# New time tables for the mixer of a streaming encoder step, with its channel layer norm rewritten

## The chip, the core and the metric

The kernel runs on one core of a Trainium2 chip. The metric is the device time of one execution, in microseconds (us). The kernel before took 3596.52 us, the median of three runs (3595.49 to 3606.69). One more execution was recorded by the profiler; the views below are of it.

## The reference, cut to what matters

```python
xn = rmsnorm(x) * norm_mix                     # 1024 prompt rows + 64 sample rows, 1024 wide, float32
u, p, q, gates = split(xn @ w_in)              # 512 | 512 | 512 | 2048
y, h = s5(u)                                   # complex diagonal state space, a scan over time
a = pa * sigmoid(qa),  pa, qa = split(gelu(y) @ w_ssm_glu)
c = depthwise_conv31(p * sigmoid(q)) + conv_b  # causal, 31 taps, 512 channels
b = silu(layernorm(c) * ln_g + ln_b) @ w_conv_out   # the norm runs over the 512 channels
x = x + (sigmoid(gA) * a + sigmoid(gB) * b) @ w_out
# channel mixer, per row of x and head (8): 2 x 128 key scores, top 16 of each, top 16 of their sums,
# softmax weights g_k; then over the 16 chosen experts k of 16384
x = x + sum_k g_k * gelu(u_tab[k] . xn2) * v_tab[k]
out = rmsnorm(x)                               # and the end states of the scan and of the convolution
```

## The kernel before, in words

The rows are taken in four groups (GROUPS): 256 prompt rows and 16 sample rows, so that the mixer works on tiles of 128 channels by 272 columns (time). Each group passes through two jobs.

**The expert job** works on tiles of 128 rows: eight of the prompt and a last one, and for each on pairs of 16-expert lists. Its unit is a turn of four experts, and a turn has two halves of two experts (BATCH = 2). GpSimd (POOL) issues one indirect DMA per expert slot (L1510: 128 rows of 8 KB, that is u_tab and v_tab of the chosen expert, into one of eight slots of rows). VectorE (DVE) forms the dot product (L1383), ScalarE (ACT) takes its gelu, multiplies by the softmax weight and writes a diagonal matrix (L915, L918, L922), and TensorE (PE) adds diag x rows into ps_acc (L765), which frees the slot (semaphore slot_free). DVE also finds the top 16 for the pair to come (choose, L1327 to L1359). A full group is 64 turns, 128 halves.

**The mixer job** makes a group's rows. Weights come as slabs of 512 KB through a ring of four that SP loads; a product (L593) is eight matmuls of 128x272 into one of two banks ps_a, emptied by ACT, or of three banks ps_v, emptied by DVE. Its pieces, in the order of the list PIECES: xn (transposes of the normed rows), u, cq and cp (the convolution's two inputs), s (into the scan), y (out of it, into the single bank ps_y), gate (16 products, ACT's sigmoid), glu, mean and var (the layer norm's two sums by matmul), cout, out, rows, q and score. A table names the half in which PE issues each piece (first dict of a Plan) and the half in which DVE, ACT or POOL take their steps (second dict): turn_in and scan (DVE), turn_back (POOL), gelu (ACT, from ps_y), tap (DVE, one of the 31 taps of the convolution on four channel tiles, L1228), centre, square, eps, root, scale, swish. Before, an emptying by ACT stands in the same half as its product.

The first group's mixer stands alone: the opening, OPEN = 60 halves without expert work (table OPENING). The mixer of each later group is laid beside the expert halves of the group before it (table STEADY; beside() calls mix() in every half). In a half PE issues its mixer piece and then the slots of two experts; ACT does its batch of two experts and then its mixer steps; DVE does its mixer steps and then the dots. Every engine runs its stream in this written order, so a wait of one step holds all that stands behind it.

The layer norm before: PE sums, DVE subtracts the mean (L1275), ACT squares (L866), PE sums again, DVE adds eps (L1279), ACT takes the root (L869), DVE the reciprocal (L1282) and multiplies (L1284); ACT's sigmoid of the scaled and shifted value goes to sq (L873), DVE repeats scale and shift (L1290) and multiplies both into cs (L1293, L1294), which cout reads.

Of the kernel before, what the change touches and what calls it, by code (L numbers as in the profile page):

```python
# [11 lines left out]
P = 128  # L12
# [18 lines left out]
TAPS = 31  # L31
# [51 lines left out]
class Plan:  # L83

    def __init__(self, pe, other, streamed):
        self.pe, self.other = pe, other
# [17 lines left out]
    def due(self, step, h):  # L104
# [6 lines left out]
     "s": [10, 12, 14, 16], "y": [14, 16, 18, 20],  # L111
     "gate": [13 + m for m in range(10)] + [31 + m for m in range(6)], "glu": [23 + j for j in range(DT)],
     "mean": [32], "var": [34], "cout": [38, 39, 40, 41], "out": [43 + j for j in range(DT)],
     "rows": [52, 53, 54], "q": [51 + m for m in range(2 * HEADS)],
     "score": [52 + m for m in range(2 * HEADS)]},
    {"cp": [7, 9, 11, 13], "turn_in": [11, 13, 15, 17], "scan": [11, 13, 15, 17], "turn_back": [11, 13, 15, 17],
     "gelu": [15, 17, 19, 21], "tap": [15 + k // 2 for k in range(TAPS)], "glu": [24 + j for j in range(DT)],
     "centre": [33], "square": [33], "eps": [35], "root": [35], "scale": [36], "swish_in": [36], "swish": [37],
     "cout": [39, 40, 41, 42], "rows": [53, 54, 55], "sq": [55], "ms2": [56], "rs": [57],
     "load_x": [60], "sq_next": [64], "ms_next": [65], "norm_next": [66]}, False)  # L120
STEADY = Plan(
    {"xn": [0], "u": [17, 19, 21, 23], "cq": [1, 5, 9, 13], "cp": [3, 7, 11, 15],
     "s": [20, 22, 24, 26], "y": [26, 28, 30, 32],
     "gate": [25 + 2 * m for m in range(10)] + [44] + [61 + 2 * m for m in range(5)],
     "glu": [45 + 2 * j for j in range(DT)],
     "mean": [52], "var": [58], "cout": [71, 73, 75, 77], "out": [80 + 2 * j for j in range(DT)],
     "rows": [95, 97, 99], "q": [96 + 2 * m for m in range(2 * HEADS)],
     "score": [97 + 2 * m for m in range(2 * HEADS)]},
    {"cp": [5, 9, 13, 17], "turn_in": [22, 24, 26, 28], "scan": [22, 24, 26, 28], "turn_back": [22, 24, 26, 28],
     "gelu": [27, 29, 31, 33], "tap": [18 + k for k in range(TAPS)], "glu": [47 + 2 * j for j in range(DT)],  # L130
     "centre": [54], "square": [55], "eps": [60], "root": [61], "scale": [62], "swish_in": [63], "swish": [65],
     "cout": [73, 75, 77, 79], "rows": [97, 99, 101], "sq": [101], "ms2": [102], "rs": [104],
     "load_x": [106], "sq_next": [117], "ms_next": [119], "norm_next": [121]}, True)
# [6 lines left out]
OPEN = 60  # L140
# [32 lines left out]
def program(nc, x_prompt, x_sample, kept, first, slabs, experts, g_ffn, g_final, x2_d, rs_d, score_d, made_d,  # L173
# [5 lines left out]
    with ExitStack() as ctx:  # L179
# [139 lines left out]
        ln_sig = sem("ln_sig")  # L319
# [85 lines left out]
        def _(sp):  # L405
# [74 lines left out]
            for h in range(OPEN):  # L480
# [316 lines left out]
        def _(act):  # L797
# [198 lines left out]
        def _(dve):  # L996
# [221 lines left out]
            def tap(k):  # L1218

                taps = par("conv_w")  # L1220
                for c in range(CT):
                    src, wk = vbuf[:, c, k:k + NC], taps[:, c * TAPS + k:c * TAPS + k + 1]
                    if k == 0:
                        before[c] = mark(dve.tensor_scalar(acc[:, c, :], src, wk, par("conv_b")[:, c:c + 1],
                                                           ALU.mult, ALU.add))
                    else:
                        after(before[c])
                        last = dve.scalar_tensor_tensor(acc[:, c, :], src, wk, acc[:, c, :], ALU.mult, ALU.add)  # L1228
                        if k < TAPS - 1:
                            before[c] = mark(last)  # L1230
                if k == TAPS - 1:
                    last.then_inc(conv_ready, 1)
# [10 lines left out]
            def mix(h, g):  # L1243
# [23 lines left out]
                for tap_k in due("tap", h):  # L1267
                    tap(tap_k)
# [8 lines left out]
                for _ in due("eps", h):  # L1277
                    src = ready(v_at(g, "var"))
                    dve.tensor_scalar(lnr[0][:, 0:NC], src[:, 0:NC], EPS, None, ALU.add).then_inc(v_done, 1)  # L1279
                for _ in due("scale", h):  # L1280
                    dve.wait_ge(std_ready, g + 1)
                    step(dve.reciprocal(lnr[0][:, 0:NC], lnr[1][:, 0:NC]))  # L1282
                    for c in range(CT):
                        last = dve.tensor_tensor(acc[:, c, :], acc[:, c, :], lnr[0][:, 0:NC], ALU.mult)  # L1284
                    last.then_inc(ln_ready, 1)
                for _ in due("swish", h):
                    dve.wait_ge(ln_ready, g + 1)
                    for c in range(CT):
# [160 lines left out]
        def _(pool):  # L1449
# [172 lines left out]
```

## Time and profile before

| | |
|---|---|
| median of three runs | 3596.52 us |
| the profiled execution's own time | 3593.31 us |
| its span | 3591.5 us |
| mean granted TensorE clock | 0.97 of full speed |
| busy: PE, DVE, ACT, POOL | 3193.5, 2417.2, 1431.2, 1381.5 us |
| opening, up to the first expert gather | about 329 us |

A page of the profile gives busy times of the engines, the share of the 16 DMA engines in 40 slices, the groups of instructions that cost most, and who waited for whom. The windows view gives the same for chosen stretches; the timeline lists instructions in order, with the idle time in front of each and what ended it in brackets.

### The profile page before, as it was taken

To read this page: it belongs to the slowest core of one execution; us is meant where nothing else is said; L and a number is where in the kernel's file an instruction comes from. 1 tells how busy PE (TensorE), PEld (TensorE's weight loads), DVE (VectorE), ACT (ScalarE), POOL (GpSimd) and SP (SyncE) were. 2 spreads that over 40 slices of the span, in tenths; PEclk is the share of its full clock that TensorE was granted. 3 is DMA by queue.
4 is the path that set the end of the run, shared out by engine and by line. 5 is a ranking of instruction groups with operands and counts; after the bars stand their busy time and mean duration, and the time that the engine had idled before them with its cause. 6 is when DMAs were issued, how large, how long until landed. Compare 5 with 4: busy or idle time off the path is not lost.

```text
span 3591.5 us, 33867 instructions
## 1 busy us (share of the span) xinstructions
PE 3193.5 (89%) x10052; PEld 1819.9 (51%) x10052; DVE 2417.2 (67%) x5507; ACT 1431.2 (40%) x4220; POOL 1381.5 (38%) x1231
## 2 busy tenths in 40 slices
PE   7889998999999998999999998989999877777776
PEld 6676555555555555555655555555555322222232
DVE  6633579767656678867656588867656666666664
ACT  4312444554334345554334345553333333333332
POOL 2101345333333445434333345434343444444443
PEclk9899999999999999999999999999999999999999
DMA  4256999999999999999999998999999999999998
GB/s 135 71 170 230 382 418 343 381 415 369 418 411 408 399 411 345 392 392 392 419 405 398 401 407 336 401 386 400 418 411 400 416 419 420 396 420 401 419 381 347
DMA packets 232072, 1336.42 MB, mean 372 GB/s; under 512 B 27664, under 2 KB 49296, under 8 KB 92624
## 3 DMA queue, kind: packets, MB, share of 16 engines
q0 software_dynamic: 156672, 1140.92, 78.1%
q1 hardware_dynamic: 62992, 179.96, 13.5%
q10 hardware_dynamic: 12224, 13.38, 1.0%
q8 instruction: 80, 1.31, 0.1%
q14 instruction: 104, 0.85, 0.1%
HBM read 1310.93 MB, written 23.23 MB: 371 GB/s over the span
## 4 chain that ended last, share of the span: by engine, by line
PE 58%; DMA 21%; DVE 8%; ACT 8%; issue 4%; POOL 1%; POOLq 0%; SPq 0%; ACTq 0%; DVEq 0%
PE ps_acc L765 32%; DMA rows<-in_experts,idx 20%; PE ps_a L593 14%; PE ps_v L593 4%; PE ps_a L668 3%; DVE rows L1383 3%; ACT uy L824 2%; POOL rows L1510 1%; DVE va L1228 1%; ACT coef L918 1%; ACT diag L922 1%; PE ps_a L695 1%; PE ps_y L635 1%; ACT L915 1%; PE ps_a L672 1%
## 5 line engine op out<-in xcount | busy, mean ns | idle before, releaser
L765 PE MATMUL ps_acc<-rows,diag 128*128 128x512 f32 x4352 | 2030.9, 614 | 292.0 <-ACT diag L922 289.3
L1510 POOL DMA_INDIRECT rows<-in_experts,idx x1088 | 1257.3, 1156 | 1894.5 <-PE ps_acc L765 1529.2
L1383 DVE CUSTOM_DVE_ANT_0 rows<-rows,xn 128x1024 f32<-128x1024 f32 x1088 | 1330.1, 1232 | 827.4 <-DMA rows<-in_experts,idx 812.7
L765 PEld LDWEIGHTS ps_acc<-rows,diag 128*128 128x128 f32 x4352 | 831.2, 196 | 1335.8 <-issue 848.0
L915 ACT ACTIVATE act_v<-dots 128x2 f32<-128x2 f32 x544 | 109.6, 201 | 1161.2 <-DVE dots L1383 1150.0
L922 ACT ACTIVATE diag<-pk,coef 128x128 f32<-128x128 f32 x1088 | 377.2, 394 | 17.7
L593 PE MATMUL ps_a<-xnT,ring 128*128 128x272 f32 x1536 | 375.8, 400 | 0.9 <-ACT xnT L812 0.7
L593 PEld LDWEIGHTS ps_a<-xnT,ring 128*128 128x128 f32 x1536 | 297.4, 194 | 93.3 <-issue 34.4
L918 ACT ACTIVATE coef<-act_v,soft 128x1 f32<-128x1 f32 x1088 | 261.4, 287 | 17.8
L593 PE MATMUL ps_a<-gates,ring 128*128 128x272 f32 x1024 | 247.7, 395 | 4.4 <-issue 3.5
L1228 DVE SCALAR_TENSOR_TENSOR va<-va,pk 128x302 f32<-128x302 f32 x480 | 240.2, 564 | 1.9
L593 PEld LDWEIGHTS ps_a<-gates,ring 128*128 128x128 f32 x1024 | 194.7, 191 | 67.4 <-issue 29.1
L855 ACT ACTIVATE gates<-ps_a,pk 128x272 f32<-128x272 f32 x64 | 31.2, 488 | 281.0 <-PE ps_a L593 280.8
L593 PE MATMUL ps_v<-uy,ring 128*128 128x272 f32 x512 | 126.9, 398 | 7.6 <-DVE uy L1294 7.6
L668 PE MATMUL ps_a<-xnT,ring 128*128 128x272 f32 x512 | 130.3, 399 | 2.2 <-DVE xnT L1304 1.2
L915 ACT ACT_TABLE_LOAD x99 | 127.0, 1283 | 6.8 <-DVE dots L1383 5.1
L593 PEld LDWEIGHTS ps_v<-uy,ring 128*128 128x128 f32 x512 | 98.7, 193 | 33.5 <-DVE uy L1294 8.1
L668 PEld LDWEIGHTS ps_a<-xnT,ring 128*128 128x128 f32 x512 | 94.5, 190 | 30.9 <-issue 11.5
L1383 DVE DVE_READ_ACCUMULATOR2_ANT dots<- 128x1 f32 x1088 | 88.9, 82 | 0.0
L892 ACT ACTIVATE sig<-ps_a 128x272 f32<-128x272 f32 x64 | 25.3, 395 | 159.3 <-PE ps_a L593 159.1
L824 ACT ACTIVATE uy<-ps_a 32x68 f32<-32x68 f32 x256 | 56.0, 219 | 81.7 <-PE ps_a L593 78.9
L1487 POOL TENSOR_TENSOR rs<-rs,half 128x3 f32<-128x3 f32 x4 | 3.6, 889 | 196.7 <-DVE rs L1178 196.6
(227 smaller groups left out, 2258.9 us busy)
## 6 DMA issues: line engine op xcount, KB each, us to landing
ring<-in_slabs SPq DMA_DIRECT2D x256, 512.0 KB
rows<-in_experts,idx POOLq DMA_INDIRECT x1088
ring<-made_slabs SPq DMA_DIRECT2D x24, 512.0 KB
sc<-score_rows SPq DMA_DIRECT2D x68, 128.0 KB
score_rows<-gp ACTq DMA_DIRECT2D x32, 256.0 KB
xt<-in_x_prompt SPq DMA_DIRECT2D x4, 1024.0 KB, 14.4
x_rows<-xt ACTq DMA_DIRECT2D x4, 1024.0 KB, 10.8
x2t<-x_rows SPq DMA_DIRECT2D x8, 512.0 KB
```

Source lines behind the costliest of these rows:

```text
L593: last = pe.matmul(out[:, 0:N], w, rhs[:, k, :], start=(k == 0), stop=(k == kt - 1))
L635: last = pe.matmul(out, w, hst[:, t % 2, c, i, 0:NK], start=False, stop=(c == 1))
L668: last = pe.matmul(out[:, 0:N], ring[:, slot, k * P:(k + 1) * P], merged[:, k, :], start=(k == 0), stop=(k == DT - 1))
L672: pe.matmul(out[:, n:n + width], xt[0:width, t, j * P:(j + 1) * P], eye[0:width, 0:width], start=False, stop=False, skip_group_check=True)
L765: ins = pe.matmul(ps_acc[:, h, :], diag[:, slot, :], rows[:, slot, D + h * 512:D + (h + 1) * 512], start=False, stop=False, skip_group_che ...
L824: last = act.activation(o, x, func)
L915: act.activation(act_v[:, cols], dots[:, cols], ACT.Gelu).then_inc(gelu_done, 1)
L918: act.activation(coef[:, s:s + 1], act_v[:, s:s + 1], ACT.Copy, scale=soft[:, n % 2, s:s + 1]).then_inc(coef_done, 1)
L922: act.activation(diag[:, s % RING, :], shape, ACT.Copy, scale=coef[:, s:s + 1]).then_inc(diag_done, 1)
L1228: last = dve.scalar_tensor_tensor(acc[:, c, :], src, wk, acc[:, c, :], ALU.mult, ALU.add)
L1383: ins = dve.tensor_tensor_reduce(rows[:, slot, 0:D], rows[:, slot, 0:D], xn[:, :], 1.0, 0.0, ALU.mult, ALU.add, dots[:, s:s + 1])
L1510: pool.indirect_dma_start(out=rows[:, slot, :], out_offset=None, in_=experts, in_offset=bass.IndirectOffsetOnAxis(ap=idx[:, a, k:k + 1], a ...
```

## The change

Both tables are written anew, and four pieces of code change with them.

- **lag**: with lag = 1 (STEADY) ACT's emptyings of ps_a stand one half after their product; the opening keeps 0. xn is left as it was.
- **tap** works in 32 units: a unit is two taps on two of the four channel tiles, the first 16 units on tiles 0 and 1, the rest on tiles 2 and 3. The count of instructions stays at 124 for a group.
- **layer norm**: POOL raises var + eps to the power -0.5 (one TENSOR_TENSOR on 128x302, with half, which holds -0.5); ACT's root and DVE's reciprocal go. ACT's Silu writes cs directly, in eight instructions (four tiles, prompt and sample columns apart); ACT's four sigmoids and DVE's twelve instructions go.
- **tables**: opening: y three halves apart (was two), 13 gates ahead of glu and 3 behind (was 10 and 6), mean and var between the glu products, OPEN = 59, all from out on one half earlier. Groups: u, s and y spread over halves 9 to 36 (was 17 to 32), taps over halves 11 to 46 without the four halves of turn_in (was 18 to 48 without a gap), mean at 48 (was 52), cout at 68 (was 71), q at 93 (was 96).
- SP loads the scores of the first two lists two and four halves behind their last score piece, one list at a time (was both at the sixth q piece), and the first x2 rows at the ninth q piece (was the eighth).

```diff
-     "s": [10, 12, 14, 16], "y": [14, 16, 18, 20],
+     "s": [10, 12, 14, 16], "y": [15, 18, 21, 24],
...
-                if h == OPENING.pe["q"][5]:
-                    for b in range(2):
+                for b in range(2):
+                    if h == OPENING.pe["score"][2 * b + 1] + 2:
                         sp.wait_ge(score_out[b], 32)
                         load_scores(0, b)
-                if h == OPENING.pe["q"][7]:
+                if h == OPENING.pe["q"][8]:
...
             def mix(h, g):
-                at, due = plan(g).at, plan(g).due
-                for _ in at("xn", h):
+                due = plan(g).due
+
+                def at(piece, h):
+                    return plan(g).at(piece, h - plan(g).lag)
+
+                for _ in plan(g).at("xn", h):
...
-                for _ in due("root", h):
-                    v_emptied(v_at(g, "var"))
-                    act.activation(lnr[1][:, 0:NC], lnr[0][:, 0:NC], ACT.Sqrt).then_inc(std_ready, 1)
-                for _ in due("swish_in", h):
+                for _ in due("swish", h):
+                    act.wait_ge(y_done, CT * (g + 1) + 2)
                     act.wait_ge(ln_ready, g + 1)
                     for c in range(CT):
-                        act.activation(sq[:, c, :], acc[:, c, :], ACT.Sigmoid, bias=par("ln_b")[:, c:c + 1],
-                                       scale=par("ln_g")[:, c:c + 1]).then_inc(ln_sig, 1)
+                        out, shape = by_step(cs[:, c, :]), (par("ln_b")[:, c:c + 1], par("ln_g")[:, c:c + 1])
+                        act.activation(out[:, :, 0:KP], in_time(acc[:, c, 0:NP]), ACT.Silu, bias=shape[0], scale=shape[1])
+                        act.activation(out[:, :, KP:NK], in_time(acc[:, c, SOFF:NC]), ACT.Silu, bias=shape[0],
+                                       scale=shape[1]).then_inc(cs_ready, 1)
...
+            def tap(unit, g):
+                taps, (two, first) = par("conv_w"), divmod(unit, 16)
+                if first == 0:
+                    emptied(v_at(g, "cp", 2 * two + 1))
+                for k in range(2 * first, min(2 * first + 2, TAPS)):
+                    for c in (2 * two, 2 * two + 1):
...
+                for _ in plan(g).due("root", h):
+                    pool.wait_ge(var_ready, g + 1)
+                    pool.tensor_tensor(lnr[1][:, 0:NC], lnr[0][:, 0:NC], half[:, 0:1].to_broadcast([P, NC]),
+                                       ALU.pow).then_inc(std_ready, 1)
```

On PE in the opening, from one y piece (L632, L635) to the next, before: the last instructions of a y, two gate products, the next y, which waits for the gelu of the one ahead (y_gelu).

```order
L635 MATMUL ps_y<-hst,rows 128x68 x2
L593 MATMUL ps_a<-xnT,ring 128x272 [waits slab_in3,a_done]
L593 MATMUL ps_a<-xnT,ring 128x272 x7
L593 MATMUL ps_a<-xnT,ring 128x272 [waits slab_in0,a_done]
L593 MATMUL ps_a<-xnT,ring 128x272 x7
L632 MATMUL ps_y<-uy,rows 128x68 [waits wt_done,unrotated,y_gelu]
L635 MATMUL ps_y<-hst,rows 128x68 x2
```

The same place after, where the lines are L635, L638 and L596:

```order
L638 MATMUL ps_y<-hst,rows 128x68 x2
L596 MATMUL ps_a<-xnT,ring 128x272 [waits slab_in1,a_done]
L596 MATMUL ps_a<-xnT,ring 128x272 x7
L596 MATMUL ps_a<-xnT,ring 128x272 [waits slab_in2,a_done]
L596 MATMUL ps_a<-xnT,ring 128x272 x7
L596 MATMUL ps_a<-xnT,ring 128x272 [waits slab_in3,a_done]
L596 MATMUL ps_a<-xnT,ring 128x272 x7
L635 MATMUL ps_y<-uy,rows 128x68 [waits wt_done,unrotated,y_gelu]
L638 MATMUL ps_y<-hst,rows 128x68 x2
```

Between two y pieces there are now three gate products, and no longer two.

On ACT in the opening, from the last two gates ahead of the layer norm's root to the first out piece (L877), before:

```order
L855 ACTIVATE gates<-ps_a,pk 128x272 [waits a_ready] x2
L869 ACT_TABLE_LOAD
L869 ACTIVATE hst<-hst 128x302 [waits v_done]
L855 ACT_TABLE_LOAD
L855 ACTIVATE gates<-ps_a,pk 128x272 [waits a_ready]
L873 ACTIVATE gp<-va,pk 128x302 [waits ln_ready]
L873 ACTIVATE gp<-va,pk 128x302 x3
L877 ACTIVATE gates<-ps_a 128x272 [waits a_ready]
```

And after, from the gates that stand ahead of Silu (L879, L880):

```order
L862 ACTIVATE gates<-ps_a,pk 128x272 [waits a_ready] x2
L879 ACT_TABLE_LOAD [waits ln_ready]
L879 ACTIVATE uy<-va,pk 128x4x64 [waits y_done]
L880 ACTIVATE uy<-va,pk 128x4x4
L879 ACTIVATE uy<-va,pk 128x4x64
L880 ACTIVATE uy<-va,pk 128x4x4
L879 ACTIVATE uy<-va,pk 128x4x64
L880 ACTIVATE uy<-va,pk 128x4x4
L879 ACTIVATE uy<-va,pk 128x4x64
L880 ACTIVATE uy<-va,pk 128x4x4
L862 ACT_TABLE_LOAD
L862 ACTIVATE gates<-ps_a,pk 128x272 [waits a_ready]
```

The root and its table load are gone; eight Silu instructions with a table of their own write uy (cs), and one gate follows them.

On DVE in a later group, a turn_in and scan (rot, rin, into, gp) and what follows, before:

```order
L1197 TENSOR_TENSOR rin<-rot 128x272 [waits v_done]
L1199 TENSOR_TENSOR into<-carry,decay 128x16 [waits unrotated]
L1203 TENSOR_TENSOR rin<-rin,into 128x8x2 [waits v_chain]
L1212 SCALAR_TENSOR_TENSOR gp<-decay,none,rin 128x272 [waits unrotated,v_chain]
L1212 SCALAR_TENSOR_TENSOR gp<-decay,none,rin 128x272
L1228 SCALAR_TENSOR_TENSOR va<-va,pk 128x302 [waits v_chain] x4
L1375 RECIPROCAL inv<-den 128x2 [waits exp_done]
L1376 TENSOR_TENSOR soft<-ex,inv 128x32 [waits v_chain]
L1383 ISA rows,dots<-rows,xn 128x1024 [waits landed0]
```

And after, the same steps of a later group:

```order
L1204 TENSOR_TENSOR rin<-rot 128x272 [waits v_done]
L1206 TENSOR_TENSOR into<-carry,decay 128x16 [waits unrotated]
L1210 TENSOR_TENSOR rin<-rin,into 128x8x2 [waits v_chain]
L1219 SCALAR_TENSOR_TENSOR gp<-decay,none,rin 128x272 [waits score_out1,unrotated,score_out0,v_chain]
L1219 SCALAR_TENSOR_TENSOR gp<-decay,none,rin 128x272
L1386 ISA rows,dots<-rows,xn 128x1024 [waits landed4]
L1386 ISA dots 128x1
L1386 ISA rows,dots<-rows,xn 128x1024 [waits landed5]
L1386 ISA dots 128x1
L1238 SCALAR_TENSOR_TENSOR va<-va,pk 128x302 [waits v_chain] x4
```

Before, a tap (L1228) stood in the same half as each turn_in; now the half goes on with what the expert job has there, and the next unit of taps comes a half later.

## Rows read from the trace of the kernel before

**Rows 1.** The page, part 1: busy us (share of the span) x instructions.

```profile
PE 3193.5 (89%) x10052; PEld 1819.9 (51%) x10052; DVE 2417.2 (67%) x5507; ACT 1431.2 (40%) x4220; POOL 1381.5 (38%) x1231
```

**Rows 2.** Windows: stretch, length, busy of each engine, PE clock, DMA share, GB/s.

```profile
103.00:165.00 62.00, 48.83 (x184) 41.12 (x184) 35.59 (x75) 21.25 (x62) 6.12 (x8) 0.75 0.17 54
...
430.00:530.00 100.00, 95.04 (x297) 54.52 (x296) 73.51 (x175) 40.88 (x132) 41.12 (x36) 1.00 1.01 419
530.00:670.00 140.00, 123.03 (x438) 76.60 (x438) 121.78 (x259) 73.62 (x221) 68.76 (x68) 0.93 0.91 346
...
790.00:850.00 60.00, 52.09 (x151) 29.09 (x150) 41.17 (x95) 29.83 (x66) 21.05 (x20) 0.94 0.92 360
...
2750.00:3570.00 820.00, 617.01 (x1341) 248.96 (x1340) 540.65 (x1215) 264.04 (x877) 375.13 (x312) 0.97 1.00 408
```

**Rows 3.** Timeline of the opening, PE: start, length, instruction [idle before, ended by].

```profile
90.08 7.55 PE L593 MATMUL ps_a<-xnT,ring 128*128 128x272 f32 x32
...
103.19 0.69 PE L632 MATMUL ps_y<-uy,rows 128*128 128x68 f32 x2 [3.83 <-ACT uy L824]
...
108.37 9.97 PE L593 MATMUL ps_a<-xnT,ring 128*128 128x272 f32 x32
123.89 0.69 PE L632 MATMUL ps_y<-uy,rows 128*128 128x68 f32 x2 [5.56 <-ACT uy L824]
...
165.03 2.10 PE L593 MATMUL ps_a<-uy,ring 128*128 128x272 f32 x8 [1.89 <-ACT uy L824]
...
228.34 17.08 PE L593 MATMUL ps_v<-uy,ring 128*128 128x272 f32 x64 [7.63 <-DVE uy L1294]
...
314.43 0.93 PE L695 MATMUL ps_a<-pk,sig 128*128 128x128 f32 x6
...
319.06 0.93 PE L695 MATMUL ps_a<-pk,sig 128*128 128x128 f32 x6
```

**Rows 4.** Timeline of the opening, ACT.

```profile
118.37 0.49 ACT L855 ACTIVATE gates<-ps_a,pk 128x272 f32<-128x272 f32 x1 [3.18 <-PE ps_a L593]
118.88 1.28 ACT L824 ACT_TABLE_LOAD   x1
120.17 3.67 ACT L824 ACTIVATE uy<-ps_y 32x68 f32<-32x68 f32 x16
```

**Rows 5.** Timeline of the opening, DVE.

```profile
73.10 0.44 DVE L1191 TENSOR_TENSOR rot<-ps_v,trig 128x272 f32<-128x272 f32 x1 [1.09 <-PE ps_v L617]
...
76.01 1.46 DVE L1212 TENSOR_TENSOR_SCAN gp<-decay,none,rin 128x272 f32<-128x272 f32 x2
...
221.44 1.62 DVE L1284 TENSOR_TENSOR va<-va,hst 128x302 f32<-128x302 f32 x4
...
318.82 0.30 DVE L1327 MAX8 topv<-sc 128x8 f32<-128x128 f32 x1 [8.31 <-DMA sc<-score_rows]
```

**Rows 6.** Lines of POOL, by form: count | busy us, mean ns | idle before.

```profile
L1467 POOL TENSOR_TENSOR gp<-gp,trig 128x272 f32<-128x272 f32 x16 | 16.8, 1049 | 0.0
...
L1487 POOL TENSOR_TENSOR rs<-rs,half 128x3 f32<-128x3 f32 x4 | 3.6, 889 | 196.7 <-DVE rs L1178 196.6
```

**Rows 7.** Timeline of POOL: the first gather.

```profile
329.28 1.19 POOL L1510 DMA_INDIRECT rows<-in_experts,idx  x1 [17.82 <-DVE idx L1359]
```

**Rows 8.** Waits from 530 to 670 us: total us, times, longest.

```profile
ACT gates L855 <- PE ps_a L593: 31.1, 6, 9.3
...
PE ps_y L632 <- ACT uy L824: 6.8, 3, 2.5
```

**Rows 9.** Waits from 790 to 850 us.

```profile
DVE hst L1282 <- ACT hst L869: 6.7, 1, 6.7
...
DVE va L1290 <- ACT gp L873: 5.2, 1, 5.2
```

**Rows 10.** Lines of DVE: the taps.

```profile
L1228 DVE SCALAR_TENSOR_TENSOR va<-va,pk 128x302 f32<-128x302 f32 x480 | 240.2, 564 | 1.9
```

**Rows 11.** Source view of L1279, eps, in the mixers of groups three and four.

```profile
L1279 DVE TENSOR_SCALAR hst<-ps_v x2: 473/473/473, 1579.6 to 2382.4; 128x302 f32<-128x302 f32 x2
```

More of the change, by code:

```diff
@@ L83, with __init__ @@
 class Plan:
-    def __init__(self, pe, other, streamed):
-        self.pe, self.other = pe, other
+    def __init__(self, pe, other, streamed, lag):
+        self.pe, self.other, self.lag = pe, other, lag
         self.a, self.v, self.slab, self.slabs = {}, {}, {}, []
@@ L110 @@
     {"xn": [0], "u": [1, 2, 3, 4], "cq": [5, 7, 9, 11], "cp": [6, 8, 10, 12],
-     "s": [10, 12, 14, 16], "y": [14, 16, 18, 20],
[L112 to L115, printed above, removed]
-    {"cp": [7, 9, 11, 13], "turn_in": [11, 13, 15, 17], "scan": [11, 13, 15, 17], "turn_back": [11, 13, 15, 17],
[L117 to L120, printed above, removed]
+     "s": [10, 12, 14, 16], "y": [15, 18, 21, 24],
@@ new lines @@
+     "gate": [13 + m for m in range(13)] + [34 + m for m in range(3)], "glu": [26 + j for j in range(DT)],
+     "mean": [29], "var": [32], "cout": [37, 38, 39, 40], "out": [42 + j for j in range(DT)],
+     "rows": [51, 52, 53], "q": [50 + m for m in range(2 * HEADS)],
+     "score": [51 + m for m in range(2 * HEADS)]},
+    {"cp": [7, 9, 11, 13], "turn_in": [11, 13, 15, 17], "scan": [11, 13, 15, 17], "turn_back": [11, 13, 15, 17],
+     "gelu": [16, 19, 22, 25], "tap": [10, 10, 12, 12, 14, 14, 16, 16] + [18 + u // 2 for u in range(24)],
+     "glu": [27 + j for j in range(DT)],
+     "centre": [30], "square": [30], "eps": [33], "root": [33], "scale": [34], "swish": [35],
+     "cout": [38, 39, 40, 41], "rows": [52, 53, 54], "sq": [54], "ms2": [55], "rs": [56],
+     "load_x": [59], "sq_next": [63], "ms_next": [64], "norm_next": [65]}, False, 0)
@@ L121 @@
 STEADY = Plan(
-    {"xn": [0], "u": [17, 19, 21, 23], "cq": [1, 5, 9, 13], "cp": [3, 7, 11, 15],
-     "s": [20, 22, 24, 26], "y": [26, 28, 30, 32],
-     "gate": [25 + 2 * m for m in range(10)] + [44] + [61 + 2 * m for m in range(5)],
+    {"xn": [0], "u": [9, 11, 21, 23], "cq": [1, 5, 13, 17], "cp": [3, 7, 15, 19],
+     "s": [12, 16, 24, 28], "y": [20, 24, 32, 36],
+     "gate": [25 + 2 * m for m in range(10)] + [44, 54] + [61 + 2 * m for m in range(4)],
      "glu": [45 + 2 * j for j in range(DT)],
-     "mean": [52], "var": [58], "cout": [71, 73, 75, 77], "out": [80 + 2 * j for j in range(DT)],
-     "rows": [95, 97, 99], "q": [96 + 2 * m for m in range(2 * HEADS)],
-     "score": [97 + 2 * m for m in range(2 * HEADS)]},
@@ L129 @@
[L129 to L133, printed above, removed]
+     "mean": [48], "var": [54], "cout": [68, 70, 72, 74], "out": [77 + 2 * j for j in range(DT)],
@@ new lines @@
+     "rows": [94, 96, 98], "q": [93 + 2 * m for m in range(2 * HEADS)],
+     "score": [95 + 2 * m for m in range(2 * HEADS)]},
+    {"cp": [6, 10, 18, 22], "turn_in": [14, 18, 26, 30], "scan": [14, 18, 26, 30], "turn_back": [14, 18, 26, 30],
+     "gelu": [21, 25, 33, 37],
+     "tap": [11, 12, 13, 15, 16, 17, 19, 20, 21, 22, 23, 24, 25, 27, 28, 29] + [31 + u for u in range(16)],
+     "glu": [48 + 2 * j for j in range(DT)],
+     "centre": [51], "square": [52], "eps": [57], "root": [57], "scale": [60], "swish": [61],
+     "cout": [70, 72, 74, 76], "rows": [96, 98, 100], "sq": [101], "ms2": [102], "rs": [104],
+     "load_x": [106], "sq_next": [117], "ms_next": [119], "norm_next": [121]}, True, 1)
@@ L139 @@
 SKEW = 4
-OPEN = 60
+OPEN = 59
 ALL_TURNS = TILES * TPAIRS * PTURNS + SPAIRS * PTURNS
@@ L318, in program @@
         neg_rs = sem("neg_rs")
-        ln_sig = sem("ln_sig")
+        var_ready = sem("var_ready")
         cs_ready = sem("cs_ready")
@@ L1216, in _ @@
             before = [0] * CT
[L1218 to L1231, printed above, removed]
+            def tap(unit, g):
[4 more added lines that the diff above has]
+                    for c in (2 * two, 2 * two + 1):
+                        src, wk = vbuf[:, c, k:k + NC], taps[:, c * TAPS + k:c * TAPS + k + 1]
+                        if k == 0:
+                            before[c] = mark(dve.tensor_scalar(acc[:, c, :], src, wk, par("conv_b")[:, c:c + 1],
+                                                               ALU.mult, ALU.add))
+                        else:
+                            after(before[c])
+                            last = dve.scalar_tensor_tensor(acc[:, c, :], src, wk, acc[:, c, :], ALU.mult, ALU.add)
+                            if unit < 31 or k < TAPS - 1:
+                                before[c] = mark(last)
+                if unit == 31:
                     last.then_inc(conv_ready, 1)
@@ L1266, in mix @@
                     scan(t, g)
-                for tap_k in due("tap", h):
-                    tap(tap_k)
+                for unit in due("tap", h):
+                    tap(unit, g)
                 for j in due("glu", h):
```

19 lines of the change are left out of this document (6 added, 13 removed).

## Prediction

> **What bounds the kernel now.** I read the page first [rows 1]: PE is busy for 89% of the span, DVE for 67%. That names no bound, since the stages differ. The windows do [rows 2]. From 430 to 530 us the DMA engines stand at a share of 1.01 with 419 GB/s: the expert gathers and the slabs fill them, and no engine's work counts there. From 2750 us on, where only experts are left, it is the same (1.00): 312 gathers in 820 us are 2.63 us each. So time can be won only where the DMA engines are not full. There are two such places. The first is the opening, up to the first gather at 329.28 us [rows 7]. The second recurs in each of three groups: 530 to 670 us at a share of 0.91, and 790 to 850 us at 0.92. Against 1.01 these lose 140 x 0.10 = 14.0 us and 60 x 0.09 = 5.4 us, 19.4 us a group.
>
> The timelines of the opening say what it waits for: PE, and PE for ACT. In front of a y piece PE stands 3.83 or 5.56 us [rows 3], because ACT first empties the gate ahead (0.49), loads a table (1.28) and does the gelu (3.67) [rows 4]: 0.49 + 1.28 + 3.67 and the hand-overs make 5.56. After it PE is slow: from 103 to 165 us the granted clock is 0.75 in the mean [rows 2], some of it at the lower of the two levels (1.2 and 2.4 GHz). Two gate products took 9.97 us after a 3.83 us idle and 7.55 us before it [rows 3], 2.4 us more, and the y between (103.19 to 108.37, 5.18 us) about double, 2.6 us more. So an idle of that size costs itself and 5.0 us. The idle of 1.89 us at 165.03 cost nothing more: eight instructions took 2.10 us, as fast as any.
>
> **The opening, part by part.** A y now comes every three halves with three gate products between. The gelu starts behind the second, and the third (7.55 / 2, about 3.7 us) covers it but for 5.56 - 3.7, about 1.9 us. The y pieces start behind three gelus, so three idles of 1.9 us; the fourth gelu stands behind the last gate and glu waits the full 5.56 us. Idle before: y 3.83, 5.56, 5.56 (one row stands for two) and glu 1.89, 16.8 us; after 3 x 1.9 + 5.56 = 11.3. The slow spells behind the three long idles go (15.0), one comes behind the glu idle (5.0). Three gates move from behind glu to ahead (11.1).
> First glu: 165.03 - 16.8 + 11.3 - 15.0 + 11.1 = 155.6 us.
> From there to cout 63.3 us before (228.34 - 165.03). Three gates fewer: -11.1. Slow spell: +5.0. The idle ahead of cout, 7.63 us, becomes what the new layer norm leaves open. Behind var PE has one glu and three gates, 4 x 3.7 = 14.8 us. Beside them runs eps (0.47), the power P, four multiplies (1.62) [rows 5], a table load (1.28), which waits for the multiplies, and eight Silus, which I put at 3 us from the gate row of 0.49 for 272 columns, plus 0.4 for hand-overs: P + 6.8. ACT's own way (second last gate emptied, table, Silu) is 3.7 + 7.4 + 0.5 + 1.3 + 3.0 = 15.9. So the idle is 1.1 us up to P = 9 and P - 8 beyond.
> P is the unknown. No row shows a power over 302 columns. The near rows are 0.889 us for a power over 3 columns and 1.049 us for a product over 272 [rows 6]. If all but the product's rate per column is fixed cost, P = 0.9 + 302 x 1.049 / 272 = 2.1 us. If the 3 columns carry the whole, P = 302 x 0.889 / 3 = 89 us. The two rows stand equally near, so I take a value between, 10 us, and keep both ends. Idle 2.1 us, so -5.5.
> First cout: 155.6 + 63.3 - 11.1 + 5.0 - 5.5 = 207.3 us, 21.0 earlier. The couts took 17.08 us for 64 instructions behind the 7.63 us idle, against 7.55 / 32 x 64 = 15.1 [rows 3]; that 2.0 comes back too. From out on nothing changes but SP: the first list's scores are fetched behind the fifth q piece, not the sixth, and a q piece with its score takes 319.06 - 314.43 = 4.6 us. DVE waited for that fetch 8.31 us to 318.82 [rows 5], and the first gather hangs on it [rows 7]. So 4.6 more. The second list's fetch is 9.2 us behind the first, and DVE needs 10.5 us for the first list (318.82 to 329.28), so it is not late. x2's fetch goes later by one q piece and now runs beside gathers; the first landed rows, up to 8 x 2.63 us of them, cover it.
> Opening: 21.0 + 2.0 + 4.6 = 27.6 us. What hides the taps: 32 of 124 stand ahead of the last scan, which can't start before the last s piece ends (99.4, where the 3.83 us idle begins) and takes 4.4 (73.10 to 76.01 + 1.46 [rows 5]). The other 92 at 0.564 us [rows 10] take 52 us, to 156; mean comes behind four glus, near 175.
>
> By the Trainium skill (ScalarE: Activation LUTs, What ACT_TABLE_LOAD costs) a switch of tables costs a drain of 1.38 us behind the load's 1.28. Here the gelu starts 1.29 us behind its load's start [rows 4], so no drain shows. By the page Silu's switch would end 1.4 us later, and the forecast would be 1.4 us more.
>
> **The groups.** From 530 to 670 us ACT waited 31.1 us for gate products of its own half, up to 9.3 at once, and PE 6.8 us for gelus [rows 8]: y, gelu and y two halves apart held each other. With lag 1 a product stands a whole half ahead of its emptying, and y four halves apart, so both waits go. DVE is late next, being 121.78 us busy of 140 [rows 2]. Its expert work is 540.65 / 156 = 3.47 us a half (312 gathers are 156 halves); a tap step adds 4 x 0.564 = 2.26, turn_in with scan 4.4. Halves 18 to 33 before: 16 x (3.47 + 2.26) + 4 x 4.4 = 109.3 us, 6.83 a half. Halves 14 to 30 after, 13 of 17 with a tap unit: 59.0 + 29.4 + 17.6 = 106.0, 6.23 a half. A half lasts (2382.4 - 1579.6) / 128 = 6.27 us [rows 11]. The excess was 16 x 0.56 = 9.0 us and goes to nothing: 9.0 of the 14.0 come back. The rest stays with DVE, which is still nearly full.
> From 790 to 850 us DVE stood 6.7 us for ACT's root and 5.2 for its sigmoids [rows 9], both held behind a gate that PE had still to make. Root and reciprocal go, eps to scale has three halves (18.8 us), Silu needs no DVE. The power holds POOL for P; the gathers behind it wait, but eight slots in flight last 8 x 2.63 = 21 us. I take 3.2 of the 5.4 back. DVE's new wait for the last gate ahead of cout has two halves of slack; behind it stand the dots. 12.2 us a group, 36.6 for three; between 0 and all 19.4.
>
> **Sum.** 3593.3 - 27.6 - 36.6 = 3529.1 against the profiled execution. The median of the runs shown is 3.2 us above it, so 3532 us.
>
> **Rivals.**
> A, only the opening gains. For it: DVE is as full as before, and PE was 123.03 us busy of 140 at a clock of 0.93; a window's loss may be PE's and stay. Against: the waits in rows 8 and 9 are queue waits. 3532 + 36.6 = 3569 us.
> B, slower: the power costs by the column. Place: POOL, in the opening and in front of the gathers in each group. With 89 us, the opening's idle is 81 instead of 2.1 (+79), and each group loses 89 - 21 = 68 us beyond what the slots cover (+204): 3815 us. It decides from P where (P - 10) + 3 x (P - 21) eats the 64 us: P = 34 us, 0.11 us a column. For it: 0.889 us is long for 3 columns. Against: such a time over so few columns looks like fixed cost. The Trainium skill (GPSIMD Engine Reference, 3.1 Elementwise) says to leave elementwise work to VectorE, with 2.6 cycles a column for two inputs; it has no price for a power. Its direction is B's, and the product row, 1.049 us, is all this trace has on it.
> C, three idles of 1.9 us lower the clock as those of 3.83 did: 15 us of the opening's gain stay away, 3547 us. Against it stands the one 1.89 us idle.
> D, the groups get all 19.4 us: 3532 - 21.6 = 3510 us. The wait for PE and for DVE would both have to vanish.
>
> **How the numbers follow.** Forecast 0.54, A 0.17, B 0.11, C 0.10, D 0.08. A measurement can tell 0.3%, 10.8 us, from no change, so below 3585.7 is faster. Forecast, C and D are; of A, 0.01 is lost to a power of 20 to 30 us in it; that and the near side of B give 0.04 for the same, and 0.11 for slower: faster 0.85. The likeliest's own range, with a P of 2 to 20 us and groups of 7 to 17 us each, is 3510 to 3556. The range 3500 to 3585 takes in A, C and D and leaves out B.
>
> **What would show it.** Right: the first gather near 301 us; PE's idles ahead of y near 1.9 us with the gates between at full clock; glu near 156 and cout near 207 us; POOL's power near 10 us; the two stretches at a DMA share of 0.97 or more, and eps steps some 790 us apart instead of 803. Wrong: a power above 34 us; ACT still waiting for ps_a in the groups; a share that stays at 0.91 with DVE full; an idle ahead of cout above 5 us.

## The result: slower, and the profile after

The changed kernel takes 3684.1 us (median of 4 runs, 3679.6 to 3689.0) against 3596.0 (3591.3 to 3606.7): a ratio of 1.024, interval 1.022 to 1.026. The forecast was 3532 us. The profiled execution took 3688.98 us, its span 3687.2.

The page of the changed kernel, parts 1 and 5, with columns as in [rows 1, 10]:

```profile
PE 3178.9 (86%) x10052; PEld 1806.4 (49%) x10052; DVE 2403.1 (65%) x5455; ACT 1447.7 (39%) x4241; POOL 1599.7 (43%) x1235
...
L1238 DVE SCALAR_TENSOR_TENSOR va<-va,pk 128x302 f32<-128x302 f32 x480 | 256.3, 598 | 2.7
L1497 POOL TENSOR_TENSOR hst<-hst,half 128x302 f32<-128x302 f32 x4 | 196.2, 49046 | 78.2 <-DVE hst L1289 78.2
```

Only POOL has much more to do than in [rows 1], 218 us more, and four powers of 49.05 us each are 196 of them. The waits of DVE (total us, times, longest) say who paid:

```profile
DVE rows L1386 <- DMA rows<-in_experts,idx: 824.8, 609, 4.4
DVE va L1295 <- POOL hst L1497: 182.1, 4, 46.5
```

This is how it looks in a group, first on POOL, then on DVE (timelines around 790 us; L1517 is the gather, L1497 the power, L1289 eps, L1295 the scale):

```profile
793.44 0.93 POOL L1517 DMA_INDIRECT rows<-in_experts,idx  x1 [0.31 <-issue]
794.38 49.57 POOL L1497 TENSOR_TENSOR hst<-hst,half 128x302 f32<-128x302 f32 x1
844.15 1.19 POOL L1517 DMA_INDIRECT rows<-in_experts,idx  x1 [0.20 <-issue]
```

```profile
788.43 0.47 DVE L1289 TENSOR_SCALAR hst<-ps_v 128x302 f32<-128x302 f32 x1
...
843.99 1.62 DVE L1295 TENSOR_TENSOR va<-va,hst 128x302 f32<-128x302 f32 x4 [45.56 <-POOL hst L1497]
```

The power begins 5.95 us after eps does. DVE is at the scale at 843.99 - 45.56 = 798.43 us, 4.05 us later: that is all of the power that DVE doesn't wait for there. The stages, as in [rows 2]:

```profile
350.00:370.00 20.00, 8.38 (x41) 6.50 (x40) 9.85 (x32) 2.14 (x5) 7.75 (x8) 0.84 1.01 401
...
390.00:410.00 20.00, 20.00 (x77) 12.80 (x76) 1.36 (x4) 6.48 (x22) 3.75 (x4) 1.00 1.00 401
410.00:430.00 20.00, 20.00 (x74) 12.35 (x73) 16.46 (x35) 8.36 (x27) 13.05 (x7) 1.00 0.80 275
430.00:530.00 100.00, 94.08 (x296) 53.96 (x295) 69.88 (x159) 46.24 (x144) 43.58 (x40) 0.97 0.99 397
530.00:670.00 140.00, 135.51 (x499) 83.76 (x498) 131.54 (x290) 76.51 (x236) 73.29 (x68) 0.99 0.97 395
...
790.00:850.00 60.00, 17.04 (x47) 8.76 (x46) 11.52 (x28) 7.70 (x19) 57.27 (x7) 0.67 0.24 87
```

The crowded stretch of 530 to 670 us has risen from a DMA share of 0.91 to 0.97, as forecast. That of 790 to 850 us has fallen from 0.92 to 0.24: while POOL raises to the power, no gather is issued and every other engine runs dry. Eps steps of the groups stand (2436.8 - 788.4) / 2 = 824.2 us apart, not 790.

The opening on PE, the steps of [rows 3]; below it the first gather on POOL, for [rows 7]:

```profile
100.34 7.55 PE L596 MATMUL ps_a<-xnT,ring 128*128 128x272 f32 x32
109.78 0.44 PE L635 MATMUL ps_y<-uy,rows 128*128 128x68 f32 x2 [1.89 <-ACT uy L827]
...
114.04 13.00 PE L596 MATMUL ps_a<-xnT,ring 128*128 128x272 f32 x48
...
163.95 4.00 PE L596 MATMUL ps_a<-uy,ring 128*128 128x272 f32 x8 [5.56 <-ACT uy L827]
...
199.87 11.16 PE L596 MATMUL ps_a<-xnT,ring 128*128 128x272 f32 x48
252.79 17.29 PE L596 MATMUL ps_v<-uy,ring 128*128 128x272 f32 x64 [41.76 <-ACT uy L880]
```

```profile
350.87 1.19 POOL L1517 DMA_INDIRECT rows<-in_experts,idx  x1 [14.93 <-DVE idx L1362]
```

The idles are the forecast ones, 1.89 and 5.56 us. But the three gate products behind the first idle take 13.00 us, where the same number of instructions, 48, takes 11.16 at 199.87: they ran partly at the lower clock. And cout waits 41.76 us for the layer norm instead of 2.1.

### The profile page after: what moved, and what is told of

Same layout as the page of the kernel before. It is cut to its first block, busy times and chain, and to the rows that moved or that the text cites. A ratio compares the mean times of both kernels' runs of the same rounds, so it can differ in the third digit from the quotient of the medians.

```text
span 3687.2 us, 33829 instructions
## 1 busy us (share of the span) xinstructions
PE 3178.9 (86%) x10052; PEld 1806.4 (49%) x10052; DVE 2403.1 (65%) x5455; ACT 1447.7 (39%) x4241; POOL 1599.7 (43%) x1235
## 4 chain that ended last, share of the span: by engine, by line
PE 50%; DMA 24%; DVE 9%; POOL 7%; ACT 6%; issue 4%; POOLq 0%; SPq 0%; ACTq 0%; DVEq 0%
PE ps_acc L768 27%; DMA rows<-in_experts,idx 23%; PE ps_a L596 12%; POOL hst L1497 5%; DVE rows L1386 4%; PE ps_a L671 3%; PE ps_v L596 3%; POOL rows L1517 2%; DVE va L1238 2%; ACT uy L827 1%; ACT coef L925 1%; PE ps_a L698 1%; ACT diag L929 1%; PE ps_a L675 1%; PE ps_acc L759 1%
## 5 line engine op out<-in xcount | busy, mean ns | idle before, releaser
L1517 POOL DMA_INDIRECT rows<-in_experts,idx x1088 | 1275.7, 1172 | 1805.0 <-PE ps_acc L768 1476.3
L596 PE MATMUL ps_a<-xnT,ring 128*128 128x272 f32 x1536 | 373.6, 398 | 0.9 <-ACT xnT L815 0.7
L596 PEld LDWEIGHTS ps_a<-xnT,ring 128*128 128x128 f32 x1536 | 295.7, 193 | 92.7 <-issue 34.4
L596 PE MATMUL ps_a<-gates,ring 128*128 128x272 f32 x1024 | 248.9, 397 | 18.7 <-ACT sig L899 17.9
L1238 DVE SCALAR_TENSOR_TENSOR va<-va,pk 128x302 f32<-128x302 f32 x480 | 256.3, 598 | 2.7
L596 PEld LDWEIGHTS ps_a<-gates,ring 128*128 128x128 f32 x1024 | 195.3, 192 | 83.6 <-issue 24.7
L1497 POOL TENSOR_TENSOR hst<-hst,half 128x302 f32<-128x302 f32 x4 | 196.2, 49046 | 78.2 <-DVE hst L1289 78.2
L596 PE MATMUL ps_v<-uy,ring 128*128 128x272 f32 x512 | 127.7, 399 | 41.8 <-ACT uy L880 41.8
L596 PEld LDWEIGHTS ps_v<-uy,ring 128*128 128x128 f32 x512 | 99.3, 194 | 68.0 <-ACT uy L880 42.2
L1295 DVE TENSOR_TENSOR va<-va,hst 128x302 f32<-128x302 f32 x16 | 6.5, 469 | 182.1 <-POOL hst L1497 182.1
L596 PE MATMUL ps_a<-uy,ring 128*128 128x272 f32 x256 | 65.9, 401 | 5.6 <-ACT uy L827 5.6
```

The source lines that it names most:

```text
L596: last = pe.matmul(out[:, 0:N], w, rhs[:, k, :], start=(k == 0), stop=(k == kt - 1))
L1497: pool.tensor_tensor(lnr[1][:, 0:NC], lnr[0][:, 0:NC], half[:, 0:1].to_broadcast([P, NC]), ALU.pow).then_inc(std_ready, 1)
L1517: pool.indirect_dma_start(out=rows[:, slot, :], out_offset=None, in_=experts, in_offset=bass.IndirectOffsetOnAxis(ap=idx[:, a, k:k + 1], a ...
```

## Experiments

"Root back" below means one edit on the changed kernel: ACT's Sqrt (it waits for eps) and DVE's reciprocal in place of POOL's power. The edits are shown cut to the lines that matter. The kernel before was measured again beside each set of experiments, so its median moves a little, between 3592.9 and 3596.7 us; ratios are against the one beside it.

**1. Root back.**

```diff
-                    pool.tensor_tensor(lnr[1][:, 0:NC], lnr[0][:, 0:NC], half..., ALU.pow)
+                    act.activation(lnr[1][:, 0:NC], lnr[0][:, 0:NC], ACT.Sqrt)
+                    step(dve.reciprocal(lnr[0][:, 0:NC], lnr[1][:, 0:NC]))
```

> The changed kernel with one thing undone: GpSimd's power over 302 columns goes, ACT takes the square root (waiting for eps) and VectorE the reciprocal; all of the new tables and ACT's silu stay. T1 (the power's price by column, 4 x 49.06 us, of which VectorE waits 182.1 us, is the whole loss): about 3684 - 182 + 4 x 2 (root, table load, reciprocal) = 3500 to 3520 us; both stretches without a hole; VectorE's wait ahead of scale under 5 us. R1 (the new tables themselves cost, the power only fills slack): it stays above 3596 us. R2 (clock falls behind the 1.89 us idles and x2's later fetch cost most of what the opening gains): 3530 to 3560 us, with the first gather near 310 us.

Measured 3507.3 us, 0.977 of the kernel before (0.975 to 0.979). Against 3684.1 the power costs 176.9 us, 44.2 in the mean of four places. The two traces say how it is spread: the first gather comes at 350.87 us with the power and at 310.27 without, 40.6 us, and eps steps of the groups stand 824.2 us apart with it and 776.3 without, 47.9 us a group. (That adds up to 184 us, which is what the two profiled executions are apart; the medians are 177 apart.) R1 of the expectation falls: tables, lag, taps and silu together are good for 85.6 us (3592.9 us for the kernel before).

**2. Root back, x2's rows behind the eighth q piece as before.**

```diff
-                if h == OPENING.pe["q"][8]:
+                if h == OPENING.pe["q"][7]:
```

> As the run before it (root and reciprocal back in place of the power), and x2's rows of the first group fetched behind the eighth q piece, as in the kernel before, not behind the ninth. If the late fetch is what holds ACT 14.5 us and empties VectorE from 390 to 410 us in the changed kernel: 5 to 15 us faster than the run before it, and the wait of ACT for that fetch goes to a few us. If the prediction's view holds (the fetch is covered by landed rows): the same within 3 us.

Measured 3495.6 us (3493.5 to 3498.6) against 3504.9 to 3509.4: 11.6 us for one half's difference, and the prediction's cover is refuted. With the late fetch ACT waited once for it, 14.5 us in the changed kernel (the line below) and 15.2 us in experiment 1:

```profile
ACT neg_top L911 <- DMA rst<-inverse_roots: 14.5, 1, 14.5
```

In experiment 2 the same wait is 5.7 us, and DVE's own wait for that fetch, 10.2 us in experiment 1, is gone. In the changed kernel the fetch is issued at 354.04 us, 3.2 us behind the first gather, and lands among gathers. The gap that follows (DVE 1.36 us busy from 390 to 410 us) shows in the windows above; experiment 1 has it from 350 to 370 us (1.79 us busy), and in experiment 2 DVE is 10.14 us busy in that stretch.

**3. Power over half the columns.**

```diff
-  lnr[1][:, 0:NC], lnr[0][:, 0:NC], half[:, 0:1].to_broadcast([P, NC])
+  lnr[1][:, 0:NC // 2], lnr[0][:, 0:NC // 2], half[:, 0:1].to_broadcast([P, NC // 2])
```

> The changed kernel with the power taken over 151 of the 302 columns; the other 151 columns keep what lay in the tile, so half the tokens are scaled with a wrong value. T1 (price by column, no large fixed part): one power lasts 24.7 us, and the kernel is 4 x about 24 us faster, near 3588 us; less if the last microseconds of each wait were covered. Rival (a large fixed cost, such as a code load or a switch per instruction): one power stays above 40 us and the kernel above 3660 us.

The other 151 columns keep what lay in the tile, so half the rows are scaled with a wrong value; only the time counts here. Measured 3584.6 us. Its page, part 5, and the wait of DVE:

```profile
L1497 POOL TENSOR_TENSOR hst<-hst,half 128x151 f32<-128x151 f32 x4 | 99.3, 24831 | 78.4 <-DVE hst L1289 78.3
```

```profile
DVE va L1295 <- POOL hst L1497: 85.8, 4, 22.5
```

24.83 us for 151 columns and 49.05 for 302: 0.160 us a column and some 0.6 fixed. The kernel moved 3684.1 - 3584.6 = 99.5 us for 4 x 24.2 = 96.9 us of power (the kernel before was 3.1 us faster beside this run, so 96 to 100 us): each microsecond between 24.8 and 49 counts in full. The power has no large fixed part.

**4. Old tables, power only.**

```diff
-  for _ in due("root", h): ... ACT.Sqrt
-  step(dve.reciprocal(lnr[0][:, 0:NC], lnr[1][:, 0:NC]))
+  for _ in plan(g).due("root", h): pool.tensor_tensor(..., ALU.pow)
```

> The kernel before, old tables and old sigmoid and swish, with one thing of the change: GpSimd's power in place of ACT's root and VectorE's reciprocal. T1: VectorE waits 46 us in each of four places less what the old root and its wait cost (6.7 us in a group): 3596 + 4 x 42 = about 3760 us. By the prediction's break-even (eight slots in flight cover 21 us of a power in a group, so 28 us stay in each of three, and 41 in the opening): 3596 + 125 = about 3720 us. If the cost came from the new tables and not from the power: near 3600 us.

Measured 3759.0 us, ratio 1.047 (1.044 to 1.050): +166.1 us, as T1 says (4 x 42 = 168). The prediction's own price for the cover gave 125. So the power costs its time with either table.

**5. Groups only.** Root back; old opening, new groups.

```diff
+    "y": [14, 16, 18, 20], "tap": [15 + min(u, 30) // 2 for u in range(32)]   (OPENING as before)
```

> Root and reciprocal instead of the power, the changed kernel's table for the three groups (with its lag and silu), and the opening of the kernel before (y two halves apart, layer norm steps at their old places, both lists' scores fetched behind the sixth q piece). It shares what the groups give. The whole of the tables with the root gives 97 us (3592.9 to 3495.6). Theory G (the groups give more than the prediction's 12.2 us each): 20 to 25 us a group, so 3593 - 3 x 22 = about 3527 us. By the prediction (12.2 a group): 3556 us. By its rival D (19.4 a group): 3535 us.

Measured 3517.8 us, 0.978 (0.976 to 0.980): 78.9 us, 26.3 a group, or 23.5 to 28.4 by the interval. Its eps steps stand 775.8 us apart, 24.8 less than before. All of that is more than rival D's ceiling of 19.4.

**6. Opening only.** Root back, x2's rows as in 2, old groups but for silu.

```diff
+    "y": [26, 28, 30, 32], "tap": [18 + min(u, 30) for u in range(32)], ... True, 0)   (STEADY as before)
```

> The counterpart: root and reciprocal instead of the power, the changed kernel's opening with x2's rows fetched behind the eighth q piece, and in the three groups the old order (lag 0, all taps and pieces at their old halves) except that silu takes the place of sigmoid and products. By the prediction the opening gives 27.6 us and the groups 0 to 3: about 3565 us. If the groups gave more than predicted, the opening's share may be as predicted: 3560 to 3570 us. If the clock's falls behind the 1.89 us idles take 7 us of it: about 3572 us.

Measured 3570.1 us, 0.993 (0.990 to 0.995): 26.6 us, or 18.7 to 34.5 by the interval. The first gather comes at 308.41 us, 20.9 earlier than before [rows 7], so 26.6 may be a little high. Eps steps stand 800.4 us apart (800.6 before), so silu by itself gives the groups nothing. With experiment 5 it makes 105.5 us; both at once (experiment 2) gave 97 to 101, so they nearly add up.

**7. Without lag.** As 2, with one number changed.

```diff
-     "load_x": [106], "sq_next": [117], "ms_next": [119], "norm_next": [121]}, True, 1)
+     "load_x": [106], "sq_next": [117], "ms_next": [119], "norm_next": [121]}, True, 0)
```

> Root and reciprocal instead of the power, x2's rows behind the eighth q piece, all new tables, but in the groups the slabs' products are emptied by ACT in their own half as before (lag 0 instead of 1). If the lag is what takes ACT's wait for gate products away (280.8 us over the kernel before, 61 with the lag): that wait returns to 200 us or more, and of the groups' gain 9 us or more each goes: above 3520 us. If the gain comes from where y and the taps stand and not from the lag: within 8 us of 3495.6 us.

Measured 3596.7 us, 1.000 (0.999 to 1.001), 101 us above experiment 2. The opening keeps its gain (first gather at 308.54 us); the groups, whose eps steps now stand 807.2 us apart, lose all of theirs and 6.6 us each beyond it. The wait of ACT for gate products, in this kernel and in experiment 2:

```profile
ACT gates L862 <- PE ps_a L596: 284.0, 59, 8.7
```

```profile
ACT gates L862 <- PE ps_a L596: 61.2, 12, 8.7
```

So the lag removes that wait, not the place of y and taps. Without the lag ACT's queue also holds up PE, which waits for the experts' coefficients (diag). Over one group's period, first in experiment 2 (737 to 1511 us), then here (759 to 1568 us):

```profile
PE ps_acc L768 <- ACT diag L932: 22.3, 13, 4.1
```

```profile
PE ps_acc L768 <- ACT diag L932: 52.6, 18, 9.0
```

It is 26.7 us slower than experiment 6, whose groups have the old table and no lag either. Why the new places are worse without lag than the old ones wasn't taken apart, and the lag on the old places wasn't run: that the lag is needed is shown, that it would be enough alone is not.

**8. Four gates between two y.** As 2, in the opening y at 14, 18, 22, 26, and all from glu on two halves later.

```diff
-     "y": [15, 18, 21, 24], ... "glu": [26 + j for j in range(DT)],
+     "y": [14, 18, 22, 26], ... "glu": [28 + j for j in range(DT)],
```

> Root and reciprocal instead of the power, x2's rows behind the eighth q piece, all new tables, and in the opening y every four halves (14, 18, 22, 26) with four gate products between, not three; glu and all behind it two halves later, the same work in all. The three idles of 1.89 us ahead of y should go: 3 x 1.89 = 5.7 us. Theory C' (idles of 1.89 us lower the granted clock for the gates that follow, about 7 us over the opening): those go too, so first glu 10 to 13 us earlier than 163.95 us, and the kernel about 3484 us. If the clock doesn't depend on these idles (only on the earlier spell): glu 5.7 us earlier, about 3490 us.

Measured 3484.5 us, 0.970 (0.968 to 0.972). PE of the opening in experiment 2:

```profile
109.12 0.44 PE L635 MATMUL ps_y<-uy,rows 128*128 128x68 f32 x2 [1.88 <-ACT uy L827]
...
113.84 12.53 PE L596 MATMUL ps_a<-xnT,ring 128*128 128x272 f32 x48
...
163.25 3.99 PE L596 MATMUL ps_a<-uy,ring 128*128 128x272 f32 x8 [5.55 <-ACT uy L827]
```

and with four gates:

```profile
107.52 0.33 PE L635 MATMUL ps_y<-uy,rows 128*128 128x68 f32 x2
...
110.15 14.88 PE L596 MATMUL ps_a<-xnT,ring 128*128 128x272 f32 x64
...
148.75 3.50 PE L596 MATMUL ps_a<-uy,ring 128*128 128x272 f32 x8 [3.75 <-ACT uy L827]
```

No idle ahead of y, and four gates in 14.88 us, 3.72 each, against 4.18 behind an idle of 1.88 us. Glu comes 14.5 us earlier: 5.7 us of idles, 1.8 of a shorter idle ahead of glu, and 7.0 that only the clock can have given, as the work is the same. From 100 to 165 us the granted clock is 0.97 here, 0.86 in experiment 2. The size varies from execution to execution: from the two gates ahead of the first y to glu, with the idles taken off, the traces with three gates take 5.8 (experiment 6) to 9.2 us (experiment 11) more than those with four. And not every idle of this size costs something: behind the third one (147.43 us in experiment 2) two gate products took 7.55 us, the full clock, and in experiment 11, the same kernel, 9.84.

**9. A power that nobody waits for.**

```diff
+                    pool.wait_ge(var_ready, g + 1)
+                    pool.tensor_tensor(dead[:, :], half..., half..., ALU.pow)
```

> Root and reciprocal carry the layer norm and x2's rows are fetched behind the eighth q piece (3495.6 us so far), and GpSimd also takes a power over 302 columns at the same place behind the same wait, of constants, into a tile that nobody reads. So VectorE never waits for it, and only GpSimd's hold of the gathers is left. By the prediction's cover (eight slots in flight last 21 us): 3 x (49 - 21) = 84 us, nothing in the opening: 3580 us. If the slots cover next to nothing because GpSimd runs near the landing of rows already: 3 x 46 = 138 us: 3634 us. If the stall came from VectorE's wait and not from the gathers held back: near 3500 us.

Measured 3625.1 us, 129.5 above experiment 2 and 132.0 above the same kernel measured beside it (experiment 11): 43.2 to 44.0 for each of three groups, if the opening's power costs nothing. Its first gather is at 311.26 us, against 306.96 in experiment 2 and 310.16 in experiment 11, so 1.1 to 4.3 us may be the opening's, and a group's at least 41.7. Its eps steps stand 819.2 us apart, against 775.8 and 776.8 in those two: 42.4 to 43.4 more. Its windows from 740 us, in a group (the power begins at 746.30):

```profile
740.00:750.00 10.00, 10.00 (x25) 4.48 (x24) 9.57 (x21) 8.86 (x17) 7.50 (x3) 1.00 0.84 320
750.00:760.00 10.00, 10.00 (x32) 5.81 (x31) 4.22 (x9) 4.34 (x8) 10.00 (x1) 1.00 0.20 67
760.00:770.00 10.00, 4.15 (x18) 2.93 (x16) 0.00 (x0) 0.00 (x0) 10.00 (x1) 0.82 0.16 52
770.00:780.00 10.00, 0.00 (x0) 0.00 (x0) 0.00 (x0) 0.00 (x0) 10.00 (x1) 0.50 0.00 0
```

DVE waits for landed rows up to 46.6 us at once. So in the groups it is enough that POOL is held: that alone makes some 43 of the 47.9 us a group that the changed kernel lost. The other 5 or so go with DVE's own wait, during which landed rows lie unused; no run has that wait alone, and up to 1 us of them is a power that took 49.6 us there in two of three groups and 48.5 here. The cover by gathers in flight is 48.5 less 42 to 44, some 5 to 7 us, not 21.

**10 and 11. Experiments 8 and 2 once more, side by side.**

> The version with four gate products between two y pieces in the opening, once more, beside the one with three in the same call. If the 14.5 us by which its first glu comes earlier stay: 11 to 15 us below the version with three, 3480 to 3485 us. If given back where the DMA engines are full: under 5 us below.

> The version with three gate products between two y pieces, with root and reciprocal and x2's rows behind the eighth q piece, once more: 3495 us within 3.

Four gates: 3480.8 us, 0.968 (0.965 to 0.970); three: 3493.1 us, 0.972 (0.970 to 0.975). They are 12.3 us apart, with times that don't overlap (3475.2 to 3485.7 and 3492.4 to 3498.1). Four gates with the root is the best version: 114 us under the kernel before, measured beside it, and 203 under the changed one.

## Why the prediction was wrong, step by step

**The power, the failed step.** The prediction put P, the time of one power over 302 columns, between 2.1 and 89 us and took 10, and held against rival B that 0.889 us over three columns "looks like fixed cost". It is 49.05 us. Rival B was the right mechanism. Its bound of 89 charged the whole 0.889 to the columns; by the slope of experiment 3 only 0.48 of it is theirs. With two bounds a factor of 42 apart and nothing to choose by, 10 was a guess, and 0.11 too small a chance for the side that could cost the most. (The chances don't quite add up either: the part of B that was counted as "the same" was left in the 0.11 for slower as well.)

**The cover, second failed term.** By rival B's rule P = 49 would cost 39 + 3 x 28 = 123 us over the forecast's 10 us: 3655. Measured it is 177 (experiment 1): by the traces some 41 us in the opening and 43 to 48 in each group (experiments 1 and 9). So the opening's term was right for this P, and the groups' cover was not there. The 21 us of "eight slots in flight" counted all slots as in flight. But a gather takes 12.5 us from issue to landing in the median (experiment 1) and one lands every 2.63 us, so some 5 are in flight (an estimate from these two numbers), and the other slots then hold rows that DVE or PE works on. The DMA share is down to 0.20 in the window from 3.7 us behind the power's start (experiment 9). The three halves (18.8 us) from eps to scale failed too: POOL reached the power 5.95 us behind eps, its gathers waiting for slots first, and DVE came to the scale 4.05 us later. The break-even can be estimated from experiment 3: 4.11 us of kernel for each microsecond of P (99.5 / 24.2), 8.3 us left at 24.83 (3592.9 - 3584.6), so P = 26.8 us, 0.089 us a column. The prediction had 34.

**The opening, near in size for a sum with wrong terms.** Forecast 27.6, measured 26.6 (18.7 to 34.5), but only with x2's rows fetched early (experiment 6). Two of its terms missed. That "the first landed rows" cover x2's later fetch was false: as the change has it, the fetch costs 11.6 us (experiment 2), so the opening as written gives 15.0. And that idles of 1.9 us cost nothing more was false; rival C had the mechanism, at 7.0 us instead of 15 (experiment 8). The first glu, forecast at 155.6 us, came at 163.95, 8.4 us late, and those 7.0 us are most of it. With the root back cout starts at 212.6 us (forecast 207.3), and the first gather comes at 306.96 us in experiment 2 and at 310.16 in experiment 11, the same kernel (forecast 301.7). These 5 to 8 us are about what the clock took before glu. The idle ahead of cout, 2.47 us (forecast 2.1), agrees by luck: the 2.1 was P = 10 less 8, and this kernel has no power. With the root back the sum's floor of 1.1 us holds, and silu at 4.3 us instead of 3 adds nearly all of the rest.

**The groups, mechanism right and size too small.** Forecast 12.2, ceiling 19.4, measured 26.3 (experiment 5). The 3.2 us taken for the second stretch had no working at all. The ceiling was read from two windows. The whole period from one eps to the next would have shown more; here it is for the kernel before, and for experiment 2:

```profile
781.00:1582.00 801.00, 755.50 (x2430) 440.46 (x2429) 565.39 (x1285) 352.97 (x1013) 321.70 (x291) 0.97 0.98 396
```

```profile
737.00:1511.00 774.00, 746.65 (x2424) 436.68 (x2424) 559.10 (x1270) 360.26 (x1023) 321.67 (x290) 0.98 1.00 408
```

801 us at 396 GB/s are 317 MB. At the 408 GB/s of the stretch of experts alone [rows 2] they take 777 us, 24 less. Eps steps now stand (2288.1 - 736.6) / 2 = 775.8 us apart, 800.6 before. That "the rest stays with DVE" was wrong: with the lag the stretch from 530 to 670 us stands at 1.00 with DVE 124.1 us busy, as full as in [rows 2]. (The groups start some 22 us earlier here; the same stretch moved by that, 508 to 648 us, stands at 1.00 too.)

```profile
530.00:670.00 140.00, 135.00 (x480) 82.69 (x479) 124.10 (x277) 84.24 (x221) 67.47 (x61) 1.00 1.00 407
```

That DVE had been busy 87% of it was no bound. What let it go faster is argued, not shown: ACT no longer waits for gate products ahead of the experts' coefficients, and PE's wait for those is 22.3 us a period with the lag and 52.6 without (experiment 7).

**The sum again, in measured terms.** 3596.0 - 78.9 (groups) - 26.6 (opening) + 11.6 (x2's fetch) + 176.9 (power) = 3679 us, against 3684.1. The forecast had 36.6, 27.6, 0 and 2.1 - 1.1 = 1 in these places, so the power alone is more than the whole miss of 152 us, and the groups' larger gain hid part of it. Right were the sign of the groups' and the opening's gain and the lag as a cause of the groups'. Silu's eight instructions last from 208.28 to 212.53 us in experiment 2, 4.3 us where 3 were taken.

## What to carry to other kernels

Where one unknown duration lies between bounds that are far apart and sits on an engine that also issues the transfers, a value between them is no forecast: most of the range from 2.1 to 89 us lay above the break-even, and the chance of "slower" should have said so. What covers a held issuing engine is what is in flight at that moment, not the number of slots. The room for gain in a loop that is bound by its transfers is its bytes over the best rate for a whole period, not the dips of the windows that catch the eye.

## What the runs showed of the hardware

A power on GpSimd over 128 partitions costs 0.160 us a column (0.889 us at 3 columns, 24.83 at 151, 49.05 at 302), while a product of 272 columns takes 1.049 us [rows 6]: a column of power costs some 40 times a column of product. ACT's root over the same 302 columns takes 0.46 us behind a table load of 1.28 (the lines below, from experiment 2), DVE's reciprocal 2.03:

```profile
197.78 1.28 ACT L876 ACT_TABLE_LOAD   x1
199.08 0.46 ACT L876 ACTIVATE hst<-hst 128x302 f32<-128x302 f32 x1
```

Behind an idle of 1.9 us ahead of y, part of PE's next work ran at the lower of the two clock levels (12.5 to 13.8 us for 48 instructions, 11.16 at the full clock). An idle of the same size at 165.03 us in the kernel before had no such effect [rows 3], nor had the first one in experiment 6 (11.21 us for the 48) and the third one in experiment 2, though that one had an effect in experiment 11, which is the same kernel. What tells them apart isn't settled here; with no such idles (experiments 8 and 10) the gates between the y pieces ran at the full clock each time.
